# A hybrid decoder layer on one core: convolution inputs and gates, gated values and output gates projected as heads and rests

## The reference, cut to what matters

```python
h = rms_norm(x, norm_mix[l])
z = h @ w_in[l]                       # (512, 1024) @ (1024, D_IN)
(g_q, g_k, g_v, g_lr, g_r, d_q, d_k, d_v, i_q, i_k, i_w, c_u) = split(z)
# gated linear attention of g_q, g_k, g_v, normalised, times silu(g_r)
# sparse attention of d_q, d_k, d_v over the 128 keys that i_q, i_k, i_w select
# c_u = (a, g): a * sigmoid(g), causal depthwise convolution of 31 taps, LayerNorm, silu
x = x + concatenate([o_gla, o_dsa, o_conv]) @ w_out[l]
```

## Time and profile before

| | |
|---|---|
| median of 3 runs | 1617.05 us (1616.18 to 1622.75) |
| the profiled execution | 1610.85 us, its span 1608.8 us |
| instructions | 19743 |
| mean granted TensorE clock | 0.968 of full speed |
| busy: TensorE, weight loads | 1515.0 us, 1043.2 us |
| busy: VectorE, ScalarE, GpSimd | 1170.7 us, 850.0 us, 510.1 us |

### The profile page before, as it was taken

How to read it: one execution, slowest core, us unless ns; L and a number is a source line. 1 busy time by engine, 2 the same in 40 slices (tenths; PEclk the granted TensorE clock), 3 DMA queues, 4 the chain that set the end, 5 groups by cost and what they waited for, 6 DMA issues and landing times. The chain is left out here.

```text
span 1608.8 us, 19743 instructions
## 1 busy us (share of the span) xinstructions
PE 1515.0 (94%) x6478; PEld 1043.2 (65%) x6478; DVE 1170.7 (73%) x1728; ACT 850.0 (53%) x1236; POOL 510.1 (32%) x224
## 2 busy tenths in 40 slices
PE   7999999999898999999899999999998899999996
PEld 3587565545566888777546865655455578878773
DVE  2697599541458999999736965985315599999996
ACT  4642323531537878788464513236125387888881
POOL 3042123100003656553532421321000036665444
PEclk9999989999979999999899999999998899999998
DMA  6243301314017999999641440103140189999995
GB/s 226 76 105 134 114 1 53 131 55 157 1 53 270 390 398 398 399 398 399 234 163 40 106 142 1 53 1 131 55 157 1 72 308 397 398 399 399 399 400 189
DMA packets 151770, 313.74 MB, mean 195 GB/s; under 512 B 33191, under 2 KB 46413, under 8 KB 151517
## 3 DMA queue, kind: packets, MB, share of 16 engines
q1 hardware_dynamic: 140300, 271.39, 46.5%
q0 software_dynamic: 6912, 25.17, 4.2%
q10 hardware_dynamic: 4496, 16.40, 2.5%
HBM read 288.81 MB, written 29.50 MB: 198 GB/s over the span
## 5 line engine op out<-in xcount | busy, mean ns | idle before, releaser
L1806 POOL TENSOR_TENSOR rest_w_down<-arena,head_w_down 128x2048 fp32r<-128x2048 f32 x30 | 192.2, 6406 | 190.3 <-ACT head_w_down L1955 190.3
L2049 DVE TENSOR_TENSOR rest_w_down<-arena,head_w_down 128x2048 fp32r<-128x2048 f32 x30 | 152.0, 5066 | 13.4 <-ACT head_w_down L1955 13.3
L645 PE MATMUL ps<-hT,arena 128*128 128x512 f32 x352 | 161.4, 599 | 0.0
L2049 DVE TENSOR_TENSOR rest_w_gate<-arena,head_w_gate 128x2048 fp32r<-128x2048 f32 x62 | 141.2, 2278 | 11.6 <-remote 11.6
L2049 DVE TENSOR_TENSOR rest_w_up<-arena,head_w_up 128x2048 fp32r<-128x2048 f32 x64 | 143.4, 2280 | 0.4 <-ACT head_w_up L1955 0.4
L1955 ACT ACTIVATE head_w_down<-arena 128x2048 fp32r<-128x2048 f32 x60 | 115.0, 1926 | 38.5 <-DMA arena<-in_w_down 38.4
L1955 ACT ACTIVATE head_w_gate<-arena 128x2048 fp32r<-128x2048 f32 x60 | 114.8, 1917 | 38.3 <-DMA arena<-in_w_gate 37.7
L1955 ACT ACTIVATE head_w_up<-arena 128x2048 fp32r<-128x2048 f32 x64 | 121.9, 1944 | 9.8 <-DMA arena<-in_w_up 9.8
L1740 POOL DMA_INDIRECT xg<-hrows,slot_tok x2 | 4.2, 2120 | 366.0 <-DVE slot_tok L1726 366.0
L1850 PE MATMUL ps<-head_w_gate,xg_head 128*128 128x512 f32 x256 | 105.2, 411 | 9.4 <-DVE xg_rest L2055 9.1
L645 PEld LDWEIGHTS ps<-hT,arena 128*128 128x128 f32 x352 | 63.4, 191 | 68.5 <-issue 67.5
(11 more groups left out here) (334 smaller groups left out, 3381.0 us busy)
## 6 DMA issues: line engine op xcount, KB each, us to landing
arena<-in_w_gate SPq DMA_DIRECT2D x64, 1024.0 KB, 10.2
arena<-in_w_up SPq DMA_DIRECT2D x64, 1024.0 KB, 11.1
arena<-in_w_down SPq DMA_DIRECT2D x64, 1024.0 KB, 10.4
arena<-in_w_in SPq DMA_DIRECT2D x10, 1536.0 KB, 6.7
yrows<-yb ACTq DMA_DIRECT2D x30, 512.0 KB, 6.2
arena<-in_w_in SPq DMA_DIRECT2D x4, 2048.0 KB, 7.7
x<-in_x SPq DMA_DIRECT2D x8, 512.0 KB, 13.6
arena<-in_w_in SPq DMA_DIRECT2D x16, 256.0 KB, 4.6
```

Of the source, the lines that this page charges most:

```text
L645: last = nc.tensor.matmul(ps[n % 2][0:width, :], w[:, c, col:col + width], hT[:, c, :], start=(c == 0), stop=(c == KD - 1))
L1806: nc.gpsimd.tensor_tensor(wl[2][:, c, :], raw[2][:, c, :], wh[2][:, c, :].bitcast(F32), ALU.subtract)\
L2049: nc.vector.tensor_tensor(wl[q][:, c, :], raw[q][:, c, :], wh[q][:, c, :].bitcast(F32), ALU.subtract)\
```

## The change

- The chunks 6, 7 and 8 (ca, cg, gv, gr) are projected as heads and rests too; plain are only ik and iq. The heads are made and kept in pieces: ca, cg, gv in two (its contraction parts 0 to 4 and 5 to 7), gr in three.
- hT_rest moves into hT's own place. So it can be made only when the last plain projection (iq) is done; on GpSimd it comes after the rests of dq and dk. The heads of dk get another place and are made by ScalarE after the third iq evacuation, ahead of the indexer's relus.
- x stays away until gr is done (before: until the last of gk).
- LENGTH is lowered for the split kinds. VALUED and GATES name steps: by the new lengths VALUED = 9, GATES = 6, FACTORED and FIRST_TAP 4 (5 before).
- Two idle products at the end of the layers' border are dropped.

```diff
+        hT_head, hT_rest = heads_at("hT_head", x_at, KD, S), heads_at("hT_rest", place_of_hT, KD, S)
+        late, soon = slots_at + 4 * (up + 7168), slots_at + 4 * (up + 3072)
+        w_head = dict(dq=heads_at("dq_head", late, KD, 512), dk=heads_at("dk_head", soon, KD, 512),
+                      dv=heads_at("dv_head", late, KD, 512), g=heads_at("g_head", soon, KD, 512),
+                      ca=heads_at("ca_head", place_of_sq, KD, CC), cg=heads_at("cg_head", soon, KD, CC),
+                      gv_a=heads_at("gv_head_a", place_of_sq, 5, GH * GV), gv_b=heads_at("gv_head_b", soon + 4 * KD * CC, 3, GH * GV),
+                      gr0=w_rest[8 % NSLOT][:, :, 384:512], gr1=heads_at("gr1_head", place_of_rs, KD, P),
+                      gr2=heads_at("gr2_head", place_of_sq, KD, P))
+        HEADS = ["rows", "dq", "dk", "dv", "g", "ca", "cg", "gv_b", "gv_a", "gr0", "gr1", "gr2"]
+        RESTS = ["dq", "dk", "rows", "dv", "g", "ca", "cg", "gv_b", "gv_a", "gr0", "gr1", "gr2"]
...
-            LENGTH = dict(ca=0.87, cg=0.87, gr=0.87, gv=0.65, kt=0.6, upd=0.7, o=1.5)
+            LENGTH = dict(ca=0.69, cg=0.69, gr=0.69, gv=0.52, kt=0.6, upd=0.7, o=1.5)
...
+            VALUED, GATES = step_of(done("gv") - 1), step_of(done("gv") - 1) - 3
...
-                    sp.wait_ge(sN["proj_done"], BEFORE_STEPS)
+                    w = A["w_out"][bass.ds(l, 1)].rearrange("o (c p) n -> p (o c) n", p=P)
+                    sp.wait_ge(sN["proj_done"], done("gv"))
+                    sp.dma_start(view(arena, SLOT, 4, D), w[:, GC:GC + 4, :]).then_inc(sN["wor_in"], 16)
+                    sp.wait_ge(sN["proj_done"], done("gr"))
                     for t in range(NT):
                         rows = xrows[P * t:P * t + P, :] if l else A["x"][0, P * t:P * t + P, :]
                         sp.dma_start(x[:, t, :], rows).then_inc(s_xt[t], 16)
...
+                        if c == 0:
+                            pe.wait_ge(sN["heads_in"], HEADS.index(of) + 1)
+                            pe.wait_ge(sN["rests_in"], max(RESTS.index(of), RESTS.index("rows")) + 1)
...
# ScalarE
+                    def head(of, chunk, c=slice(0, KD), at=None):
+                        at = slice(0, LOADED[chunk]) if at is None else at
+                        dst = w_head[of][:, :, 0:at.stop - at.start]
                         act.wait_ge(s_w[k_of(chunk)], chunks_loaded(chunk))
+                        nc.scalar.activation(dst, chunk_at(chunk)[:, c, at], ACT.Copy).then_inc(sN["heads_in"], 1)
...
                     for n in range(done("ik") + 1, AFTER_IDX):
                         evacuate(n)
+                        if n == AFTER_IDX - 2:
+                            head("dk", 3)
...
-                    chunk_head(1)
...
+                    act.wait_ge(sN["sum_done"], 6)
+                    head("ca", 6, at=slice(0, CC))
...
                         turned(n)
+                        if n == 0:
+                            act.wait_ge(sN["proj_done"], done("gk"))
+                            head("cg", 6, at=slice(CC, 2 * CC))
+                        if n == 1:
+                            head("gv_b", 7, c=slice(5, KD))
...
                         for job in ended_in(n):
                             evacuate(job)
+                            if job == done("ca") - 1:
+                                head("gv_a", 7, c=slice(0, 5))
+                        if n == GATES:
+                            head("gr0", 8, at=slice(0, P))
+                        if n == VALUED + 1:
+                            act.wait_ge(sN["proj_done"], done("gv"))
+                            head("gr1", 8, at=slice(P, 2 * P))
+                        if n == VALUED + 2:
+                            head("gr2", 8, at=slice(2 * P, 3 * P))
...
# GpSimd
-                    rows_rest()
-                    chunk_rest(0)
+                    rest("dq", 2)
+                    rest("dk", 3)
+                    gp.wait_ge(sN["proj_done"], AFTER_IDX)
+                    gp.wait_ge(sN["heads_in"], 1)
+                    nc.gpsimd.tensor_tensor(hT_rest[:, :, :], hT[:, :, :], hT_head[:, :, :].bitcast(F32), ALU.subtract)\
+                      .then_inc(sN["rests_in"], 1)
...
-                    for m in range(1, len(SPLIT)):
-                        chunk_rest(m)
+                    rest("dv", 4)
+                    rest("g", 5)
+                    rest("ca", 6, at=slice(0, CC))
...
                         do(nc.gpsimd.tensor_tensor(bm[:, n % 2, w0:P * (i + 1)], sel[:, i, w0:P * (i + 1)],
                                                    toep[:, h, 2 * P - P * near:2 * P], ALU.add), "bm_done")
+                        if n == 2:
+                            rest("cg", 6, at=slice(CC, 2 * CC))
+                        if n == 3:
+                            rest("gv_b", 7, c=slice(5, KD))
+                        if n == 4:
+                            rest("gv_a", 7, c=slice(0, 5))
+                        if n == GATES + 2:
+                            rest("gr0", 8, at=slice(0, P))
+                        if n == VALUED + 3:
+                            rest("gr1", 8, at=slice(P, 2 * P))
+                        if n == VALUED + 4:
+                            rest("gr2", 8, at=slice(2 * P, 3 * P))
...
                         row_turned(pe, 3)
-                        idle_products(2)
```

More of the change, by code:

```diff
@@ L275, in program @@
         scratch = lay("scratch", [P, 7680])
+        place_of_hT = place[0]
         hT = lay("hT", [P, KD, S])
-        place_of_mixg = place[0]
         mixg = lay("mixg", [P, GH, S])
@@ L281, in program @@
         sel = lay("sel", [P, NT, S])
+        place_of_sq = place[0]
         sq = lay("sq", [P, 2, S])
+        place_of_rs = place[0]
         rs = lay("rs", [P, 2, S])
@@ L479, in program, with weights_of @@
             NJ = len(JOBS)
+            def weights_of(name, i):
+                return {"gq": "g", "gk": "g", "gv": "gv_a", "gr": f"gr{i}"}.get(name, name)
             def k_of(chunk):
@@ L611, in _, with split_part @@
                     pe.wait_ge(sN["rows_hA"], NT)
-                    def split_project(n):
+                    def split_part(n, c):
                         chunk, col, width, kind, name, i = JOBS[n]
[L616 to L629, removed]
@@ new lines, in split_part @@
+                        of, at = weights_of(name, i), slice(col, col + width)
+                        if c == 0:
+                            pe.wait_ge(sN["heads_in"], HEADS.index(of) + 1)
+                            pe.wait_ge(sN["rests_in"], max(RESTS.index(of), RESTS.index("rows")) + 1)
+                        wl = w_rest[k_of(chunk)][:, c, at]
+                        if name == "gv":
+                            wh = w_head["gv_a"][:, c, :] if c < 5 else w_head["gv_b"][:, c - 5, :]
+                        elif name == "gr":
+                            wh = w_head[of][:, c, :]
+                        else:
+                            first = CC if name == "cg" else 0
+                            wh = w_head[of][:, c, col - first:col - first + width]
@@ new lines, in split_part @@
+                        if kind == "T":
+                            o, hh, hl = ps[n % 2][0:width, :], hT_head[:, c, :], hT_rest[:, c, :]
+                            pairs = ((wh, hh), (wl, hh), (wh, hl))
+                        else:
+                            tile = slice(P * i, P * i + P)
+                            o, hh, hl = ps[n % 2][:, 0:width], hT_head[:, c, tile], hT_rest[:, c, tile]
+                            pairs = ((hh, wh), (hh, wl), (hl, wh))
+                        for a, (lhs, rhs) in enumerate(pairs):
+                            last = nc.tensor.matmul(o, lhs, rhs, start=(c == 0 and a == 0), stop=(c == KD - 1 and a == 2))
@@ L631, in project @@
+                        return last
                     def project(n, chunks=range(KD)):
@@ L924, in _ @@
                         if n == 2:
-                            chunk_head(2)
-                    chunk_head(3)
+                            act.wait_ge(sN["proj_done"], done("dq"))
+                            head("dv", 4)
+                    act.wait_ge(sN["proj_done"], done("dk"))
+                    head("g", 5)
                     evacuate(AFTER_IDX + 6)
```

45 lines of the change are left out of this document (12 added, 33 removed).

## The result

| | before | after |
|---|---|---|
| median | 1616.62 us (1616.18 to 1622.75, 4 runs) | 1682.71 us (1678.03 to 1683.16, 4 runs) |
| profiled execution, span | 1610.85, 1608.8 us | 1678.03, 1675.9 us |
| mean granted TensorE clock | 0.968 | 0.941 |

What follows compares the result with a forecast made beforehand. VectorE limits the indexer stretch and steps 5 to 22, TensorE the projections and steps 0 to 4. Terms sum to 24.6 us per layer, twice less 0.5: +48.7, profiled 1659.6, median 1665; range 1631 to 1690 us.

Steps and rivals of the forecast that it cites:

- rival 2: Steps 3 to 11: half clock after each wait as long as the earlier one, up to 8 us per layer; 1682, chance 0.14.
- 1.2 + 3.1: VectorE's 1024-wide subtraction (1.2 us) and about four tap-sized operations (3.1) done one step earlier, in waiting time: -4.2 us.
- 1659.6 + 6.2: Predicted profiled execution, 1659.6 us, plus the 6.2 by which the median of runs is higher; forecast 1665.
- hold of the indexer's stretch: Indexer's accumulations: GpSimd's subtractions for dk and the rows hold VectorE for their whole length, +10.2 us per layer.
- the three waits on the keys: Steps 2, 6, 10: TensorE waits for level keys queued behind gv_a, gr0, gr1 rests; +4.6, +4.7, +5.2 us per layer.
- cg's 0.9: Step 1: cg's rests on GpSimd hold the normalisation until 161, +0.9 us, counted in the first key wait.
- half clock behind them: After the three key waits: TensorE's granted clock falls to near half, +4 us per layer, bounds 0 and 12.
- gain -6.2: Steps 5 to 20: VectorE work done a step earlier (-4.2) and 2 us of its idle time back, -6.2 per layer.
- gr2's rests +2.1: Attention steps: gr2's rests (1024 elements, 2.2 us) on GpSimd fall among VectorE's taps, +2.1 us per layer.
- rival 3: Indexer's stretch: GpSimd's long rests give way to VectorE's short operations, price 0 there; 1608 or 1584, chance 0.06.
- Rival 1: Level-key waits don't bind because ScalarE's heads come earlier; the indexer hold stays; 7.6 us per layer, 1632, chance 0.15.
- x comes back later: x's 2 MB return after gr is hidden by attention outputs, last steps and the mixer's tail; no cost.

Runs made afterwards that it cites:

- dots_clear: Changed kernel with dk's rests moved behind the indexer's accumulations and the rows' rests left out (same-shape product instead, less exact): 1660.53 us.
- keys_first: Changed kernel with GpSimd's level_keys of a step moved ahead of the rest() calls of the same step: 1638.25 us.
- filler: Changed kernel with 4, 6 and 7 idle TensorE products in front of its waits for the level keys of steps 2, 6 and 10: 1663.47 us.
- before_fill: Kernel before the change with two idle TensorE products in front of the turn of step 6: 1622.68 us, 1.0047 of before.
- both_late: Same as both, but with FACTORED and FIRST_TAP one step later (5, as before the change): 1642.85 us.
- both: Changed kernel with level_keys ahead of the rests, rows' rests made by VectorE, dk's rests after the accumulations: 1626.26 us, 1.0048 of before.
- both_few: Same as both, plus idle products before the indexer's products (four) and the turns of steps 17 and 18 (1 and 3): 1623.27 us, 1.0029 of before.
- oldlen_fill: Same as both, but with LENGTH as before the change, plus idle products at eight turns and before the indexer's products: 1629.21 us.

## Why the prediction was right, and where its sizes were off

The forecast was 1665, the result 1682.71: slower as said, inside the range, at its upper end. The measured time is rival 2's number, 1682, and that is in part luck. Rival 2 put the half clock at up to 8 us a layer above the sum; it was 5.6 above it. The rest of the difference is 3.8 us of gain that didn't come and 0.9 of the hold, less 1.9 by which the waits were smaller. The forecast's own arithmetic adds little: 1.2 + 3.1 is 4.3 and not 4.2, and 1659.6 + 6.2 is 1665.8. By the terms of the sum, per layer:

| term | predicted | measured, and by what |
|---|---|---|
| hold of the indexer's stretch | 10.2 | 10.7 by masked sum 0; 11.1 by dots_clear |
| the three waits on the keys, with cg's 0.9 | 14.5 | 12.6, keys_first less filler |
| half clock behind them | 4 | 9.6, filler |
| gain -6.2, gr2's rests +2.1 | -4.1 | -0.3, what is left of 33.1; the runs around the medians spread by more than that |

*The hold* was right in mechanism and size: GpSimd in the rows' rests from 62.0 to 70.8 (predicted 61.3 to 70.2), accumulations ending at 88.4 (predicted near 88). The rule of the Trainium skill that I had weighed (SBUF — State Buffer, "Who interferes with whom": an exclusion for the whole instruction, decided by the order of issue) agrees with 8.79 us under 8.81; rival 3, that GpSimd gives way, is out. GpSimd's subtraction began at 61.98, VectorE's accumulation at 62.15.

*The waits* came where they were put, behind gv_a, gr0 and gr1 at n = 4, 8 and 12. Predicted as growth between masked sums, 4.6, 4.7 and 5.2 with the clock apart; measured with it 7.2 (3 to 6), 5.8 (6 to 9) and 7.4 (9 to 12). Rival 1 is out by 44.5 us. The step-by-step chain (exponentials, head, rest, keys) was the right way to count them: the order on two queues, read in the code, gave each of them to within 1.2 us of the growth in filler, where the clock is mostly held (4.0, 3.6 and 5.1 in layer 0).

**The term that was sized most wrongly is the half clock**, taken as 4 with bounds of 0 and 12; filler gives 9.6. I had taken it low because the one in the earlier trace rows "cost VectorE nearly nothing". That was so (10.14 against 10.13 us), but it doesn't carry over to another place. In before_fill about ten microseconds of half clock, one or two steps later, cost 4.3 a layer, because VectorE waits for TensorE's logits there.

**The gain that I had left, 6.2 a layer, isn't there on balance.** both_late shows that the early work does pay against the same kernel without it (8.3 us a layer), and from masked sum 4 to 8 both does 9 taps where before does 6, in the same time (36.6 and 36.8 us). What takes it back has two parts.

- The rests hold VectorE in more places than gr2's. I had given the holds in the steps 2.1 us, and 0.9 for cg. Layer 1 of both_few, with the half clock no worse than in before, has VectorE busy for 6.8 us more (2.5 of it ahead of masked sum 4, where TensorE limits and it costs little), and 1.3 us are won where I had 6.2 less 2.1. On the page of after VectorE is busy for 29.3 us more in all, and the indexer's stretch is 19.6 of it (26.8 against 17.0 us a layer), which leaves 4.9 a layer for the steps.
- In step 18 there is a wait that I had not seen. With the lower LENGTH the planner hands out all it has by step 16 and holds the attention's outputs until 18 (FIRST_O), so step 17 is empty. TensorE is idle for 4.0 us, and the output products run at half clock (0.50 from 315 to 320) while VectorE waits 5.05 us for the logits behind them. From masked sum 18 to 20 after takes 14.8 and 14.9 us in the two layers, and before 12.0 and 14.1.

That x comes back later cost nothing that I found, as said.

## What to carry to other kernels

When work is taken off an engine that shares the limit with another, ask first what the other one does. Here TensorE had an estimated 17 us less to do in a layer, and VectorE still set the pace (51.5 us busy of 54.2 between masked sums 8 and 16). It even had more to do, as the preparations on GpSimd held it. Then ask what the lighter engine does with the time: TensorE starved, and a half clock in the wrong step cost 3 to 4.3 us; idle products moved that loss and didn't end it. Preparations for the cheaper products (heads, rests) have a place on someone's queue: put what others wait for ahead of them, as keys_first did for 44 us with one moved block. And don't lay a long two-input GpSimd instruction over a stretch in which VectorE reads two operands from SBUF and is the limit: here the stretch grew by the whole of it.

## What of the hardware was unexpected

- A VectorE accumulation of 128 elements, otherwise 0.38 us, took 8.79 us under a GpSimd subtraction of 8.81 us.
- Shorter subtractions do the same to the taps: in oldlen_fill two taps took 3.59 us with gr2's rest of 2.35 us under them, and take 1.54 without.
- Idle products that keep the granted clock at 1.00 in one place can bring the half clock on a little later. In before_fill it went from 202 to 213 us to 215 to 225, after TensorE was busy for 0.76 of 5 us (210 to 215), and the kernel got 6.3 us slower.
- Profiled runs differ by up to 3 us at the first masked sum (156.66 in both, 153.67 in both_late, whose code up to there is the same), with a half clock in the first projections (0.83 from 35 to 45 us in both, 1.00 in both_late).
